# Two of five modulation vectors summed in the norm's gap, and half of the up products in 512-column form

## The reference

```python
def modulated_norm(x, g, shift, scale):
    return rmsnorm(x, g) * (1 + scale) + shift

def swiglu(h, wg, wu, wd):
    return (jax.nn.silu(h @ wg) * (h @ wu)) @ wd          # wg, wu: 1024 x 2816, wd: 2816 x 1024

c_act = jax.nn.silu(c)                                    # c: one vector of 1024
for l in range(2):
    mod = (c_act @ w_ada[l] + b_ada[l]).reshape(b, 9, 1, 1024)
    sh1, sc1, g1, sh2, sc2, g2, sh3, sc3, g3 = [mod[:, i] for i in range(9)]
    x = x + 0.5 * g1 * swiglu(modulated_norm(x, norm_g[l, 0], sh1, sc1), ...)
    x = x + g2 * mixer(modulated_norm(x, norm_g[l, 1], sh2, sc2))
    x = x + 0.5 * g3 * swiglu(modulated_norm(x, norm_g[l, 2], sh3, sc3), ...)
```

## Time and profile before

| | |
|---|---|
| median of 3 runs | 1503.1 us (1502.41 to 1505.34) |
| profiled execution, its time | 1502.93 us |
| its span in the trace | 1501.1 us |
| mean granted TensorE clock | 0.975 |
| PE busy | 1410.7 us, 94% of the span |
| DVE busy | 898.0 us, 60% |
| ACT busy | 619.5 us, 41% |
| HBM | 380 MB moved, 253 GB/s over the span |

### The profile page before, as it was taken

The page is one execution under the profiler, slowest core; times in us unless marked ns, Lnnn a source line. Parts: engine busy times, 40 slices in busy tenths (PEclk is TensorE's granted clock), DMA queues, the critical chain, the costliest instruction groups (busy, mean ns, idle before and its releaser), DMA issues.

```text
span 1501.1 us, 26991 instructions
## 1 busy us (share of the span) xinstructions
PE 1410.7 (94%) x11552; PEld 1263.5 (84%) x11552; DVE 898.0 (60%) x1044; ACT 619.5 (41%) x740; POOL 19.1 (1%) x24
## 2 busy tenths in 40 slices
PE   7999999989999999999999999999999989995666
PEld 5999999989999989999999999999997989762223
DVE  4877775657877768777776655556557644420002
ACT  3534345555434453443444544445434643420002
POOL 0000000400000000000000000000000000000000
PEclk9999999999999999999999999999999999998779
DMA  9998867516988758788655465553635439999996
GB/s 363 323 328 300 287 251 246 152 54 245 322 302 303 258 190 313 281 299 305 206 169 169 135 209 189 175 188 123 196 96 177 158 138 350 378 420 421 420 421 271
DMA packets 204056, 380.34 MB, mean 253 GB/s; under 512 B 12741, under 2 KB 158154, under 8 KB 192202
## 3 DMA queue, kind: packets, MB, share of 16 engines
q1 hardware_dynamic: 203616, 379.08, 70.3%
q10 hardware_dynamic: 362, 0.14, 0.0%
HBM read 378.14 MB, written 1.05 MB: 253 GB/s over the span
## 4 chain that ended last, share of the span: by engine, by line
PE 82%; DMA 9%; DVE 4%; ACT 3%; issue 2%; SPq 1%; DVEq 0%; ACTq 0%
PE ps L697 18%; PE ps L699 17%; PE ps L698 17%; PE ps L725 11%; PE ps L726 5%; DMA plain_whi<-in_w_exp_down_dram 4%; PE ps L1486 2%; ACT whi L1599 2%; DMA raw<-in_w_exp_down_dram 2%; DVE wlo L2051 1%; DMA spare<-in_w_exp_down_dram 1%; DMA plain_whi<-in_w_ada_dram 1%; PE ps L1460 1%; PE ps L1444 1%; PE ps L815 1%
## 5 line engine op out<-in xcount | busy, mean ns | idle before, releaser
L2051 DVE TENSOR_TENSOR wlo<-raw,whi 128x2048 fp32r<-128x2048 f32 (+2 forms) x187 | 423.1, 2263 | 226.8 <-ACT whi L1599 226.7
L1599 ACT ACTIVATE whi<-raw 128x2048 fp32r<-128x2048 f32 (+2 forms) x187 | 352.7, 1886 | 153.6 <-PE ps L699 138.0
L697 PE MATMUL ps<-h_both,whi 128*128 128x256 f32 x1320 | 380.1, 288 | 1.0 <-DVE wlo L2051 0.9
L699 PE MATMUL ps<-h_both,wlo 128*128 128x256 f32 x1320 | 374.5, 284 | 0.0
L698 PE MATMUL ps<-h_both,whi 128*128 128x256 f32 x1320 | 374.4, 284 | 0.0
L697 PEld LDWEIGHTS ps<-h_both,whi 128*128 128x128 f32 x1320 | 251.3, 190 | 8.7 <-issue 4.1
L725 PE MATMUL ps<-h_both,whi 128*128 128x512 f32 x704 | 252.3, 401 | 0.0
L698 PEld LDWEIGHTS ps<-h_both,whi 128*128 128x128 f32 x1320 | 251.5, 191 | 0.7 <-issue 0.5
L699 PEld LDWEIGHTS ps<-h_both,wlo 128*128 128x128 f32 x1320 | 251.5, 191 | 0.0
L697 PE MATMUL ps<-hidhi,whi 128*128 128x256 f32 x704 | 201.3, 286 | 2.1 <-DVE wlo L2214 2.1
L699 PE MATMUL ps<-hidhi,wlo 128*128 128x256 f32 x704 | 199.4, 283 | 0.0
(11 more groups left out here) (352 smaller groups left out, 1867.7 us busy)
## 6 DMA issues: line engine op xcount, KB each, us to landing
ada_raw<-in_w_ada_dram SPq DMA_DIRECT2D x66, 1024.0 KB, 5.3
raw<-in_ffn_wg_dram SPq DMA_DIRECT2D x44, 1024.0 KB, 6.8
raw<-in_ffn_wu_dram SPq DMA_DIRECT2D x44, 1024.0 KB, 5.4
raw<-in_ffn_wd_dram SPq DMA_DIRECT2D x44, 1024.0 KB, 6.4
raw<-in_w_in_dram SPq DMA_DIRECT2D x18, 1024.0 KB, 5.3
raw<-in_w_in_c_dram SPq DMA_DIRECT2D x12, 1024.0 KB, 5.3
raw<-in_w_in_ab_dram SPq DMA_DIRECT2D x8, 1024.0 KB, 8.6
raw<-in_w_exp_down_dram SPq DMA_DIRECT2D x7, 1024.0 KB, 16.7
```

Of the source, the lines that this page charges most:

```text
L697: pe.matmul(o, wh, xh, start=start, stop=False, skip_group_check=shared)
L699: return pe.matmul(o, wl, xh, start=False, stop=stop, skip_group_check=shared)
L1599: act.activation(whi[s][:, 0:width], raw[s][:, 0:width], ACT.Copy).then_inc(high[s], 1)
L2051: dve.tensor_tensor(wlo[s][:, 0:width], raw[s][:, 0:width], whi[s][:, 0:width].bitcast(F32), ALU.subtract).then_inc(split[s], 1)
```

## The change

Of the five vectors of `ffn0`, `ffn1` and `ffn2` only the first three go through `ada_reduce` and `ada_turn` (EARLY = 3). The last two are weighed by DVE as before, each into an `adasum` of its own. PE sums them in the norm that follows: `vector_columns` takes eight 128 x 128 pieces of `adasum` as weights against one column of ones and so gets the vector already turned; the first of the two replaces `keep_clock(8)` between the sum of squares and the spread, the second stands behind the spread, with the fill behind it shorter by 8. DVE adds the biases in between the pieces of h (`late_mod`).

Bank 6 is thereby free from the seventh chunk on. So chunks 7 to 10 of `ffn0` to `ffn2` and chunks 1 to 10 of `ffn3` make up in `both_parts` form too (`wide_up`, banks 6 and 7): 4 + 4 + 4 + 10 = 22 of 44 chunks. ACT copies the low halves (`up_low_part`), DVE adds the high ones and then multiplies by silu (`wide_hidden`, two instructions in place of one). PE waits for the third vector's `mod_ready` ahead of the second loop of chunks. Three semaphores of early loads become one, which its waiters count.

```diff
-            def both_parts(s, k, m):
-                o = ps[:, m, :]
+            def both_parts(s, k, m, b=0):
+                o = ps[:, b + m, :]
...
+            def vector_columns(v, i, b):
+                pe.wait_ge(ada_used[1], v * 2 + 2)
+                for j in range(KT):
+                    mm = pe.matmul(ps[:, b, T // 2 + j:T // 2 + j + 1], adasum(i)[:, j * P:(j + 1) * P], ones[:, 0:1], start=True, stop=True)
+                mm.then_inc(sem("adacol_ready"), 1)
...
-                keep_clock(8)
+                if late is None:
+                    keep_clock(8)
                 own(6)
                 pe.wait_ge(sem("mod_ready"), vectors)
+                if late is not None:
+                    vector_columns(late, EARLY, 6)
                 wait("norm_rs")
...
+                if late is not None:
+                    own(7)
+                    vector_columns(late + 1, EARLY + 1, 7)
+                    freed[7] = (sem("mod_ready"), late + 2)
+                    fill = max(fill - 8, 0)
                 keep_clock(fill)
...
+                def wide_up(c):
+                    pe.wait_ge(split[1], c + b0[1] + 1)
+                    pe.wait_ge(sem("hid_done"), c + ch)
+                    for m in range(2):
+                        for k in range(KT):
+                            mm = both_parts(1, k, m, 6)
+                    mm.then_inc(used[1], 1)
...
-                if layer_v is None:
-                    nv = 0
+                early = 0 if layer_v is None else EARLY
+                if early:
+                    with pe.Fori(0, early) as i:
+                        pair(i, i + layer_v)
+                if early:
+                    pe.wait_ge(sem("mod_ready"), layer_v + early)
                 else:
-                    with pe.Fori(0, nv) as i:
-                        pair(i, i + layer_v)
-                if nv < pairs:
-                    with pe.Fori(nv, pairs) as i:
-                        pair(i)
+                    own(6)
+                with pe.Fori(early, pairs) as i:
+                    pair(i)
...
+                def up_low_part(c):
+                    act.wait_ge(used[1], c + b0[1] + 1)
+                    act.wait_ge(sem("hid_split"), c + ch)
+                    copy(hid[:, :].rearrange("p (m t) -> p m t", m=2), ps[:, 6:8, T:2 * T]).then_inc(sem("up_low"), 1)
...
+                def wide_hidden(c):
+                    dve.wait_ge(sem("up_low"), c + (wide_before[stage] - wide_from[stage] + 1))
+                    up = hid[:, :].rearrange("p (m t) -> p m t", m=2)
+                    dve.tensor_tensor(up, ps[:, 6:8, 0:T], up, ALU.add).then_inc(sem("up_summed"), 1)
+                    dve.wait_ge(sem("silu_done"), c + ch + 1)
+                    dve.wait_ge(sem("up_summed"), c + (wide_before[stage] - wide_from[stage] + 1))
+                    dve.tensor_tensor(hid[:, :], silu[:, :], hid[:, :], ALU.mult).then_inc(sem("hid_done"), 1)
...
-            norm_sums(7, 14)
+            norm_sums(5, 14, late=5)
...
-            norm_sums(13, 0)
+            norm_sums(11, 0, late=11)
...
-            norm_sums(18, 14)
+            norm_sums(16, 14, late=16)
```

More of the change, by code:

```diff
@@ L383, in build @@
         weighed = {"ffn0": 0, "ffn1": 5, "ffn2": 10}
+        wide_from = {"ffn0": 2 * EARLY + 1, "ffn1": 2 * EARLY + 1, "ffn2": 2 * EARLY + 1, "ffn3": 1}
+        wide_before = {"ffn0": 0, "ffn1": 4, "ffn2": 8, "ffn3": 12}
+        reduced = {"ffn0": 0, "ffn1": 3, "ffn2": 6}
+        behind = {"ffn0": 0, "mix0": 2, "ffn1": 2, "ffn2": 4}
         FIRST_VECTORS = (1, 0)
@@ L1718, in chunked @@
                 chunk(0, 0, down=False)
-                with act.Fori(0, (count - 2) // 2) as i:
+                narrow = (wide_from[stage] - 1) // 2
+                if narrow:
+                    with act.Fori(0, narrow) as i:
+                        for half in range(2):
+                            chunk(i * 2 + 1 + half, (1 + half) % 2)
+                with act.Fori(narrow, (count - 2) // 2) as i:
                     for half in range(2):
-                        chunk(i * 2 + 1 + half, (1 + half) % 2)
+                        chunk(i * 2 + 1 + half, (1 + half) % 2, wide=True)
                 for c in range((count - 2) // 2 * 2 + 1, count):
-                    chunk(c, c % 2, last=(c == count - 1))
+                    chunk(c, c % 2, last=(c == count - 1), wide=True)
                 for s in range(3):
@@ L2134, in _, with late_mod, norm @@
             first_vector(0)
-            def norm(gain, shift, scale=None, final=False, vectors=0, inverted=False, slot=None, after=None):
+            def late_mod(v, b):
+                dve.wait_ge(sem("adacol_ready"), v + 1)
+                sl = slice(v * KT, (v + 1) * KT)
+                dve.tensor_tensor(modv[:, sl], ps[:, b, T // 2:T // 2 + KT], bada[:, sl], ALU.add).then_inc(sem("mod_ready"), 1)
+            def norm(gain, shift, scale=None, final=False, vectors=0, inverted=False, slot=None, after=None, late=None):
                 if scale is not None:
@@ L2166, in norm @@
                         low(k - 1)
+                    if late is not None and k in (3, 4):
+                        late_mod(late + k - 3, 6 if k == 3 else 7)
                 if after:
@@ L2246, in chunked @@
                 chunk(0, 0, down=False, weigh=((0, front),) if nv else ())
-                looped = max(min(nv, pairs) - 1, 0)
+                looped = 0
                 if nv:
-                    with dve.Fori(0, looped) as i:
+                    with dve.Fori(0, EARLY - 1) as i:
                         chunk(i * 2 + 1, 1, weigh=((i, back),))
                         chunk(i * 2 + 2, 0, turn=i, weigh=((i + 1, front),))
-                    chunk(looped * 2 + 1, 1, weigh=((looped, back),))
-                    chunk(looped * 2 + 2, 0, turn=looped, last=(looped * 2 + 2 == count - 1))
-                    looped += 1
+                    for i in range(EARLY - 1, nv):
+                        chunk(i * 2 + 1, 1, weigh=((i, back),), wide=i >= EARLY)
+                        chunk(i * 2 + 2, 0, turn=i if i < EARLY else None, wide=i >= EARLY, weigh=((i + 1, front),) if i + 1 < nv else (), last=(i * 2 + 2 == count - 1))
+                    looped = nv
                 if 2 * looped + 1 < count:
```

69 lines of the change are left out of this document (39 added, 30 removed).

## The result

The changed kernel takes 1546.11 us (median of four; 1542.01 to 1547.76), the kernel before beside it 1502.93 (1502.41 to 1505.49): a ratio of 1.0279, 95% interval 1.0259 to 1.0298. The time lies above the predicted range (1517 to 1537), and the loss is 43 us where 25 were predicted. The profiled execution took 1545.24 us over a span of 1543.4, against 1502.93 before, so 42.3 us are there to be found in the traces.

The account below looks back on a forecast made before the run. PE was taken to bound the dense stages. Terms -2.6 - 2.8 + 14.7 + 4.4 + 3.7 = +17.4 us, plus clock falls of 3.6 and 4.2, made +25.2 on 1502.93: 1528 us, range 1517 to 1537.

Parts of the forecast that it names:

- wide form, 22 chunks: Up products in the dense stages: each wide chunk takes the gate's 5.65 us in place of 5.77, -2.6 us in all.
- vectors and row copy leave: Dense stages: the fourth vector's 0.94 us of PE saved in three, -2.8 us, and the row copy's 0.33 us at their ends.
- new wait with its clock: Ahead of the gate of chunk 7: PE idles for `mod_ready` in three stages, +14.7 us, plus a clock fall each, +3.6.
- chain at the ends, full clock: Ahead of down(10) in four stages: copy and addition lengthen an uncovered wait by 1.35 us each; +4.4 us net of row copies.
- norms, full clock: Norms behind ffn0, ffn1 and ffn2: one-column products delay what follows by 1.0, 1.7 and 1.0 us, +3.7 us together.
- clock at ends: Four stage ends, 2.3 to 2.4 us idle: half a clock fall of 1.2 us counted at each, part of +4.2 us.
- clock in norms: Three norms with single columns for zeros: half a clock fall of 1.2 us counted in each, part of +4.2 us.
- fourth rival: Up products go at the pace of instructions, not columns: 42 us gained in place of 2.6, 1489 us; chance 0.02.
- first rival: The clock holds everywhere: waits are as counted but no fall follows, +17.4 us, 1520 us; chance 0.12.
- The third: At `mod_ready` PE doesn't stand, the vector being stored in time: +2.7 to +6.9 us, 1506 to 1510 us; chance 0.04.
- I count half of the seven, +4.2 us: Four stage ends and three norms: a clock fall of 1.2 us follows at half of these seven places.
- second rival: The clock falls at all ten places, twice as long behind the three long waits: +33 us, 1536 us; chance 0.06.

Follow-up runs that it names:

- e3: The changed kernel with all up products in the old 256-column form and no wait for `mod_ready`, leaving little but the two late vectors in the norms: 1518.65 us.
- e6: The changed kernel with 18 products of zeros on PE in the wait ahead of down(10) of all four dense stages: 1540.16 us.
- e4: The changed kernel with the products that sum the late vectors streaming 112 columns of ones in place of one: 1534.21 us.
- e7: The changed kernel with 112 columns, the last chunk's up narrow, and the `mod_ready` wait moved to the wide up that needs bank 6: 1502.14 us, ratio 0.9990.
- e2: The changed kernel with DVE storing the third vector ahead of the split of the down weights: 1525.29 us.
- e1: The kernel before with only the vector loop cut in two and PE's wait for the third vector's `mod_ready` between: 1523.14 us, ratio 1.0133.

## Why the prediction was wrong, point by point

The direction was right, and so were the new wait, the chain at the ends and the work in the norms. The clock in the norms was mis-sized, because it was priced as if it followed idle time. The steps against what the traces and runs measured, in us:

| step | predicted | measured | from |
|---|---|---|---|
| wide form, 22 chunks | -2.6 | -2.1 | 0.097 a chunk, ffn3 of the change (0.87 in nine) |
| vectors and row copy leave | -3.8 | -3.6 | e3, within and ends |
| new wait with its clock | +18.3 | +19.4 | 6.75, 6.85, 5.81, turn to the next down against before |
| chain at the ends, full clock | +5.4 | +5.5 | e6 less e3's 0.33 |
| norms, full clock | +3.7 | +4.2 | e4, e7 |
| clock at ends | +2.4 | +4.5 | change less e6 |
| clock in norms | +1.8 | +15.1 | change less e4 |

The row copy stands with the vectors here; the last two rows are the 4.2 us of the prediction, split by places. The measured figures are together 43.0 us, near the 42.8 of the table of differences.

**The wide form** gives nearly what gate against up gave, 0.097 us a chunk in place of 0.12. A pair of gate and up takes 11.32/32 = 0.354 us after the change, where the gate's was 0.353 before. The issue gap in the Trainium skill, TensorE: Matmul & The Clock Gate, section Back-to-back issue gap, on which the prediction's estimate of 0.229 us a pair stood, is not borne out by this trace. The fourth rival, a gain at the pace of instructions, falls with the same number.

**The new wait** is 4.51 us of idle time in three places, ended by `modv`, and the gate starts 4.89 us behind the start of the turn in place of 0.17, 4.7 us later (4.9 predicted with the branch). The clock falls with each, so the first rival, that it holds, is wrong. The third, that PE doesn't stand there, is wrong too; e2 shows that with an earlier store it doesn't, though the time is then 1525 us and not 1506 to 1510, because of the ends and norms.

**The ends** are as worked out: 2.39 us of waiting against 2.3, and 1.70 and 1.36 us of loss at full clock. A fall followed at three of the four, and cost 1.5 rather than 1.2.

**The norms** are where the prediction failed. Their own work was counted well: 1.0, 1.7 and 1.0 us were predicted, and e4 lost 0.8, 2.6 and 0.8. At full clock the spread came 242.07 - 239.84 = 2.23 us after the last squares in e4, 0.6 later than before (0.5 predicted). The step that did not hold is the clock: "I count half of the seven, +4.2 us". It placed the norms between a stretch with half of PE's time idle and short waits of 1 us, gave each at most one stretch of 3.4 us at half clock, and half of that. The runs showed three stretches of 10.2, 13.7 and 10.2 us, 15.1 us of loss: ten times 3.4 us at some 1.5 each, in place of one and a half at 1.2. I had named the cause ("single columns in place of 256 columns of zeros") and priced it as if it were a short wait. The two rows of the trace from which I took the fall both stood behind idle time, and none showed a busy PE that loses its clock; with no such row, the bound from above was too low, and the range with it. The second rival, 1536 us, with a fall at all ten places, was nearest and still 10 us short, for the same reason.

What is shown is that the low clock in the norms comes with one column and goes with 112 (e4), and that no wait of the change is needed for it (e3). How many of its stretches follow is not explained.

## What to carry to other kernels

Who replaces products that fill a wait by narrow useful ones looks at the granted clock behind them, and not only at their duration: here the same products with 112 columns, 0.06 us dearer in sixteen passes, saved 12 us. A wait belongs in front of the instruction that needs the resource and not at the head of the loop that holds it: e1 pays 20 us for a line which in e7 costs nothing. An addition that is hidden in the middle of a stage is uncovered in its last chunk, and can be left out there alone.

## What the runs showed of the hardware that was not expected

In e3 PE was busy for 2.40 of 2.40 us with the last squares, the first vector's one-column products and the start of the spread, at a granted clock of 1.00 and with 0.82 us of idle time ahead, and yet the clock went to 0.50 behind them. It stayed there through windows in which PE and PEld were busy for 3.40 of 3.40 us. The same sixteen passes took 1.81 us with one column and 1.87 with 112, and with 112 the clock stayed at 1.00. At 0.50 PE did 17 or 18 products in 3.40 us in these norms, and in e4, at 1.00, 31 or 32.
